# Expert weights stored by the host in the order in which each 2 MB transfer reads them

## The chip, the cores and the metric

The kernel runs on one core of one Trainium2 chip. Its engines are TensorE (PE: matmuls; PEld: the loads of its stationary operand), VectorE (DVE), ScalarE (ACT), GpSimd (POOL) and SyncE (SP). SP and POOL issue the transfers (DMAs), and 16 DMA engines carry them out. The metric is the time of one execution on the device in microseconds (us), the median over several runs; lower is better.

## The reference

Two transformer blocks run one after the other on 512 tokens of width 1024 in fp32. The first ends in a mixture of experts, which is where the change lies:

```
logits = xt @ w_router + b_router             # 512 tokens, 32 experts
top_v, top_e = lax.top_k(logits, 4); top_w = softmax(top_v)
# the 2048 (token, expert) rows are sorted by expert, padded per expert to blocks of 128
def expert_block(tok, e):
    xb = xt[tok]                              # 128 x 1024
    g = minimum(xb @ w_gate[e] + b_gate[e], 7)
    u = clip(xb @ w_up[e] + b_up[e], -7, 7)
    act = (u + 1) * (g * sigmoid(1.702 * g))
    return act @ w_down[e] + b_down[e]
y = zeros(512, 1024).at[row_tok].add(yb * row_w)
```

Each expert has three weights of 1024 x 1024 in fp32, 4 MB each. The second block has its own mixer and then a layer that fetches, for every token, 128 rows of 8 KB from a table of 16,384 by computed indices; it is the last stage of the kernel.

## The kernel before

The program is a row of stages. In `experts` (line 1018) a loop runs over the blocks of 128 routed rows; these inputs make 36. Each engine has a loop of its own, and they meet at semaphores.

For a block, PE computes gate and up in four units u of 8 matmuls (line 1121): u = 0 is gate, columns 0 to 511; u = 1 up, the same columns; u = 2 and 3 gate and up for columns 512 to 1023. The weights of a unit lie in `wgu[:, u]`, 128 partitions x 8 x 512 fp32, 2 MB in all, 16 KB per partition. After them come the transposes of the activation (line 1126), the transposes that turn the next block's rows `xg` (line 1107), and the down projection in two halves (line 1137) out of `wd[:, 0]` and `wd[:, 1]`, again 2 MB each. DVE and ACT do bias, clamp, sigmoid and products between.

There is one buffer for each of the six weight pieces. SP refills it as soon as PE has read it for this block (`s_mm[u]`), so a load has most of a block's time until its next use. A semaphore per buffer (`s_w[u]`) holds PE until it has landed. SP issues in this order: the four of `wgu` (line 1061), the two biases (lines 1064 and 1065, 512 KB each), the two of `wd` (line 1069), the down bias (line 1071). The host's arrays are as in the reference, so partition p of a gate or up piece is gathered from 8 rows of the weight (k x 128 + p), 2 KB of each; of a down piece from 4 rows, 4 KB of each.

POOL has a chain of small transfers for each block. It scatters the 128 finished rows of 4 KB (`e_yb`, line 1097) and waits until they have landed; then it loads the row table (line 1086) and the indices of the coming block (line 1089), waits for the indices, and gathers 128 rows of 4 KB into `e_xg` (line 1076). PE waits for that gather ahead of line 1107.

After the experts, the stage `combine` (line 1202) loads the scattered rows: `c_y` in four transfers of 2 MB, 16 KB in one piece per partition (line 1224).

Of the kernel before, what the change touches and what calls it, by code (L numbers as in the profile page):

```python
# [13 lines left out]
P = 128  # L14
T = 512
NT = T // P
D = 1024
KD = D // P
W = 512
# [14 lines left out]
NE, TOPK = 32, 4  # L34
# [983 lines left out]
def experts(nc, A, K, dram, ident, mod, x, ps, blocks):  # L1018

    with ExitStack() as ctx:  # L1020
        def sb(name, shape, dt=F32):
            return ctx.enter_context(nc.sbuf_tensor("e_" + name, shape, dt))

        def sem(name):
            return take(nc, "e_" + name)

        wgu = sb("wgu", [P, 4, KD, W])
        wd = sb("wd", [P, 2, KD // 2, D])
# [12 lines left out]
        s_w = [sem(f"w{u}") for u in range(6)]  # L1041
# [9 lines left out]
        with nc.Block() as block:  # L1051
            @block.sync
            def _(sp):
                nb = sp.value_load(blocks[0:1, NBLK:NBLK + 1], min_val=1, max_val=NBLK)
                with sp.Fori(0, NBLK) as i:
                    with sp.If(i < nb):
                        e = sp.value_load(blocks[0:1, bass.ds(i, 1)], min_val=0, max_val=NE - 1)
                        for u in range(4):
                            w = A["w_up" if u % 2 else "w_gate"][bass.ds(e, 1)]
                            sp.wait_ge(s_mm[u], i + 1)  # L1060
                            sp.dma_start(wgu[:, u], w.rearrange("e (k p) n -> p (e k) n", p=P)[:, :, (u // 2) * W:(u // 2 + 1) * W]
                                         ).then_inc(s_w[u], 16)
                        sp.wait_ge(s_act, i * 2 + 1)
                        sp.dma_start(bgu[:, 0, :], A["b_gate"][bass.ds(e, 1)].broadcast_to([P, D])).then_inc(s_bgu, 16)
                        sp.dma_start(bgu[:, 1, :], A["b_up"][bass.ds(e, 1)].broadcast_to([P, D])).then_inc(s_bgu, 16)
                        for u in range(2):
                            w = A["w_down"][bass.ds(e, 1)].rearrange("e (k p) n -> p (e k) n", p=P)
                            sp.wait_ge(s_mm[4 + u], i + 1)
                            sp.dma_start(wd[:, u], w[:, 4 * u:4 * u + 4, :]).then_inc(s_w[4 + u], 16)
                        sp.wait_ge(s_y, i + 1)  # L1070
                        sp.dma_start(bd[:, :], A["b_down"][bass.ds(e, 1)].broadcast_to([P, D])).then_inc(s_bd, 16)

# [1262 lines left out]
```

## Time and profile before

| | |
|---|---|
| median of 3 runs | 4891.05 us (4889.86 to 4891.41) |
| the profiled execution | 4888.82 us, span of its trace 4887.1 us |
| PE busy | 4101.2 us (84% of the span) |
| DVE / ACT / POOL busy | 1858.0 / 701.1 / 813.0 us |
| matmuls on the `wgu` weights | 2304, 997.3 us busy |
| matmuls on the `wd` weights | 1152, 512.4 us busy |
| transfers, whole kernel | 363,917 packets, 1245.03 MB, 255 GB/s |
| weight transfers of the expert stage | 72 gate + 72 up + 72 down, 2048 KB each |

Busy time is the time in which an engine had an instruction under way; what an engine waited for stands apart. A packet is one piece moved by one DMA engine. "DMA share" is the mean busy share of the 16 engines; it can come out slightly over 1 in a short stretch. "Landing" is the time from the issue of a transfer until all of it is there. [...]

### The profile page before, as it was taken

Reading aid. Unit: us, or ns where it says so; the run is one execution under the profiler, and the core shown is the slowest. Engines: PE = TensorE matmul, PEld = TensorE weight load, DVE = VectorE, ACT = ScalarE, POOL = GpSimd, SP = SyncE. Lnnn points to the kernel's source line nnn. Section 1 sums busy time; section 2 is a strip of 40 time slices with the busy share of each in tenths; the row PEclk is TensorE's granted clock in tenths of the full one; section 3 lists DMA queues with packets and bytes.
Section 4 is the critical chain, followed back from the end, with each engine's and each line's share of the span. In section 5 each row is a group of like instructions: output and inputs, shape, how many; then the busy total and the mean of one; then the engine's idle time right before and its main releaser. Section 6 shows DMA issues by size and latency. Waiting matters only on the chain. (4 is left out here: it accounts for less than half of the span.)

```text
span 4887.1 us, 33598 instructions
## 1 busy us (share of the span) xinstructions
PE 4101.2 (84%) x10884; PEld 2003.7 (41%) x10884; DVE 1858.0 (38%) x3983; ACT 701.1 (14%) x1559; POOL 813.0 (17%) x821
## 2 busy tenths in 40 slices
PE   7689999489999999999992984897967777777777
PEld 3235544244444444444441543674423333333332
DVE  1501222412222222222224025443066676676765
ACT  0001221011111111011110111111122222222221
POOL 0000000100000000000000003000044444444442
PEclk9799999699999999999996986557989899999998
DMA  9751122099999999999974100002089999999997
GB/s 327 201 102 68 55 71 95 18 385 351 351 342 350 344 343 350 348 345 343 351 280 168 52 5 0 0 1 103 18 348 421 421 421 421 421 419 419 403 420 310
DMA packets 363917, 1245.03 MB, mean 255 GB/s; under 512 B 24663, under 2 KB 26007, under 8 KB 297376
## 3 DMA queue, kind: packets, MB, share of 16 engines
q1 hardware_dynamic: 271552, 652.07, 37.0%
q0 software_dynamic: 92256, 591.59, 30.6%
q8 instruction: 57, 0.93, 0.1%
q14 instruction: 52, 0.43, 0.0%
HBM read 1212.48 MB, written 31.20 MB: 254 GB/s over the span
## 5 line engine op out<-in xcount | busy, mean ns | idle before, releaser
L2083 PE MATMUL ps<-q_uv,q_dg 128*128 128x512 f32 x2048 | 1002.7, 647 | 324.7 <-ACT q_dg L2109 324.7
L1121 PE MATMUL ps<-e_wgu,e_xT 128*128 128x512 f32 x2304 | 997.3, 593 | 1.2 <-ACT e_xT L1145 1.2
L2083 PEld LDWEIGHTS ps<-q_uv,q_dg 128*128 128x128 f32 x2048 | 412.6, 207 | 914.2 <-issue 914.2
L2194 DVE SCALAR_TENSOR_TENSOR mod<-q_uv,mix 128x1024 f32<-128x1024 f32 x512 | 627.3, 1225 | 394.4 <-DMA q_uv<-in_peer_uv,q_picks 393.8
L2067 POOL DMA_INDIRECT q_uv<-in_peer_uv,q_picks x512 | 590.1, 1153 | 867.5 <-PE ps L2083 669.4
L1121 PEld LDWEIGHTS ps<-e_wgu,e_xT 128*128 128x128 f32 x2304 | 438.6, 190 | 553.8 <-issue 553.8
L1137 PE MATMUL ps<-e_wd,e_aT 128*128 128x512 f32 x1152 | 512.4, 598 | 24.3 <-ACT e_aT L1157 24.3
L1137 PEld LDWEIGHTS ps<-e_wd,e_aT 128*128 128x128 f32 x1152 | 212.9, 190 | 275.4 <-issue 241.1
L498 PE MATMUL ps<-hT,ring 128*128 128x512 f32 x640 | 283.1, 600 | 15.7 <-ACT qkv L617 14.2
L1196 DVE TENSOR_TENSOR e_yb<-ps,e_bd 128x1024 f32<-128x1024 f32 x36 | 44.1, 1224 | 489.3 <-PE ps L1137 489.3
L1097 POOL DMA_INDIRECT scratch_y<-e_yb,e_row x36 | 35.6, 989 | 1042.1 <-DVE e_yb L1198 1011.1
L1185 DVE TENSOR_TENSOR e_ut<-ps,e_bgu 128x512 f32<-128x512 f32 x72 | 49.8, 691 | 404.8 <-PE ps L1121 404.8
L498 PEld LDWEIGHTS ps<-hT,ring 128*128 128x128 f32 x640 | 121.2, 192 | 162.4 <-issue 161.5
L1154 ACT ACTIVATE e_sg<-e_gt 128x512 f32<-128x512 f32 x72 | 45.3, 629 | 970.7 <-DVE e_gt L1183 970.7
L1182 DVE TENSOR_TENSOR e_gt<-ps,e_bgu 128x512 f32<-128x512 f32 x72 | 49.8, 691 | 346.4 <-PE ps L1121 286.4
L2109 ACT ACTIVATE q_dg<-ident,q_w 128x128 f32<-128x128 f32 x512 | 163.6, 390 | 60.1 <-DVE q_w L2208 59.8
L238 PE MATMUL ps<-mod_ring,cB 128*128 128x512 f32 x320 | 144.8, 613 | 25.6 <-DMA mod_ring<-in_w_ada 25.6
L2103 ACT ACTIVATE q_ap<-q_ap 128x4 f32<-128x4 f32 x128 | 26.3, 205 | 957.0 <-DVE mod L2194 957.0
L1344 PE MATMUL ps<-p_ring,p_hT 128*128 128x512 f32 (+1 forms) x352 | 132.1, 538 | 0.7 <-ACT p_hT L1361 0.7
L498 PE MATMUL ps<-ring,hT 128*128 128x512 f32 x256 | 113.6, 604 | 0.7 <-ACT hT L581 0.7
L1926 PE MATMUL ps<-r_mT,r_ring 128*128 128x512 f32 x256 | 112.4, 602 | 0.7 <-ACT r_mT L1943 0.7
L238 PEld LDWEIGHTS ps<-mod_ring,cB 128*128 128x128 f32 x320 | 63.3, 198 | 106.5 <-issue 106.3
(412 smaller groups left out, 3504.1 us busy)
## 6 DMA issues: line engine op xcount, KB each, us to landing
e_wgu<-in_w_gate SPq DMA_DIRECT2D x72, 2048.0 KB, 9.7
e_wgu<-in_w_up SPq DMA_DIRECT2D x72, 2048.0 KB, 9.1
e_wd<-in_w_down SPq DMA_DIRECT2D x72, 2048.0 KB, 9.5
ring<-in_w_in SPq DMA_DIRECT2D x15, 2048.0 KB, 8.1
mod_ring<-in_w_ada SPq DMA_DIRECT2D x12, 2048.0 KB, 9.9
mod_ring<-in_w_mod SPq DMA_DIRECT2D x12, 2048.0 KB, 7.9
e_bgu<-in_b_gate SPq DMA_DIRECT2D x36, 512.0 KB, 6.9
e_bgu<-in_b_up SPq DMA_DIRECT2D x36, 512.0 KB, 9.1
```

What stands on the lines that cost most here:

```text
L238: last = nc.tensor.matmul(ps[:, g % 4, :], cB[:, v, k, :], ring[:, n % NB, k, :], start=(k == 0), stop=(k == KD - 1))
L498: last = nc.tensor.matmul(ps[:, j, :], lhs, rhs, start=(k == 0), stop=(k == kt - 1))
L1121: last = nc.tensor.matmul(ps[:, u, :], xT[:, k, :], wgu[:, u, k, :], start=(k == 0), stop=(k == KD - 1))
L1137: last = nc.tensor.matmul(ps[:, 5 + c, :], aT[:, 4 * hf + k, :], wd[:, hf, k, c * W:(c + 1) * W], start=(hf == 0 and k == 0), stop=(hf == ...
L1182: link(dve.tensor_tensor(gt[:, hf], ps[:, 2 * hf, :], bgu[:, 0, cols], ALU.add))
L1185: link(dve.tensor_tensor(ut[:, hf], ps[:, 2 * hf + 1, :], bgu[:, 1, cols], ALU.add))
L1344: last = nc.tensor.matmul(ps[:, m % 8, 0:rhs.shape[1]], lhs, rhs, start=(k == 0), stop=(k == KD - 1))
L1926: last = nc.tensor.matmul(ps[:, m % 8, :], ring[:, n % NB, k, j * P:(j + 1) * P], mT[:, k, :], start=(k == 0), stop=(k == KD - 1))
L2067: pool.indirect_dma_start(out=uv[:, n % NR, :, :].rearrange("p a d -> p (a d)"), out_offset=None, in_=A["peer_uv"], in_offset=bass.Indirec ...
L2083: last = nc.tensor.matmul(acc(t)[:, c, :], dg[:, n % ND, :], uv[:, n % NR, 1, c * W:(c + 1) * W], start=first, stop=last_one)
L2109: act.activation(dg[:, n % ND, :], ident[:, :], ACT.Copy, scale=w[:, k % 2, j:j + 1]).then_inc(s_dg, 1)
L2194: dve.scalar_tensor_tensor(junk[:, n % 2, :], uv[:, n % NR, 0, :], 1.0, h3[:, k // PH, :], ALU.mult, ALU.mult, accum_out=ap[:, k % 2, j:j ...
```

## The change

The host stores the expert weights in the order in which the kernel's transfers want them. The gate and up weights become one array `w_in_exp` of [32 experts, 4 units, 128 partitions, 4096], the down weights `w_out_exp` of [32, 2 halves, 128, 4096]. Each of the six loads of a block then reads 16 KB in one piece for each partition. Sizes, buffers, semaphores, the order of issue and all arithmetic stay as they are.

```
-                            w = A["w_up" if u % 2 else "w_gate"][bass.ds(e, 1)]
+                            w = A["w_in_exp"][bass.ds(e, 1)].rearrange("e u p n -> p (e u) n")
                             sp.wait_ge(s_mm[u], i + 1)
-                            sp.dma_start(wgu[:, u], w.rearrange("e (k p) n -> p (e k) n", p=P)[:, :, (u // 2) * W:(u // 2 + 1) * W]
+                            sp.dma_start(wgu[:, u].rearrange("p k n -> p (k n)"), w[:, u, :]
                                          ).then_inc(s_w[u], 16)
...
-                            w = A["w_down"][bass.ds(e, 1)].rearrange("e (k p) n -> p (e k) n", p=P)
+                            w = A["w_out_exp"][bass.ds(e, 1)].rearrange("e u p n -> p (e u) n")
                             sp.wait_ge(s_mm[4 + u], i + 1)
-                            sp.dma_start(wd[:, u], w[:, 4 * u:4 * u + 4, :]).then_inc(s_w[4 + u], 16)
+                            sp.dma_start(wd[:, u].rearrange("p k n -> p (k n)"), w[:, u, :]).then_inc(s_w[4 + u], 16)
...
+    halves = [np.asarray(inputs.pop(n)).reshape(NE, KD, P, 2, W).transpose(0, 3, 2, 1, 4) for n in ("w_gate", "w_up")]
+    inputs["w_in_exp"] = np.stack(halves, 2).reshape(NE, 4, P, KD * W)
+    inputs["w_out_exp"] = np.asarray(inputs.pop("w_down")).reshape(NE, 2, 4, P, D).transpose(0, 1, 3, 2, 4).reshape(NE, 2, P, 4 * D)
```

The instructions of PE, DVE, ACT and POOL are the same, in the same order. On SP, in the loop over blocks of the expert stage, the loads of `wgu` read as follows (ISA is a register instruction or a wait; the last number of a DMA is its shape):

```order
 L1060 REGISTER_ALU
 L1061 ISA
-L1061 DMA e_wgu<-in_w_gate 128x8x512
-L1061 DMA e_wgu<-in_w_up 128x8x512
+L1061 DMA e_wgu<-in_w_in_exp 128x4096
 L1061 ISA
-L1061 DMA e_wgu<-in_w_gate 128x8x512
-L1061 DMA e_wgu<-in_w_up 128x8x512
+L1061 DMA e_wgu<-in_w_in_exp 128x4096
+L1061 ISA
+L1061 DMA e_wgu<-in_w_in_exp 128x4096
```

The loads stand where they stood; one more small instruction comes ahead of some of them, three in a block.

## Rows read from the trace of the kernel before

**Rows 1.** Busy time by stretch, 1030 to 2580 us (x: count)

```profile
core 0: us, PE busy (x) PEld busy (x) DVE busy (x) ACT busy (x) POOL busy (x), PEclk, DMA share, GB/s
1030.00:2580.00 1550.00, 1522.20 (x3938) 701.20 (x3936) 354.55 (x562) 168.12 (x246) 109.71 (x141) 1.00 0.94 341
```

**Rows 2.** Waits of PE, 1030 to 2580 us: us in total, times, longest

```profile
PE ps L1137 <- ACT e_aT L1157: 24.3, 36, 0.7
```

**Rows 3.** Timeline of PE, one block: start us, us, engine, line

```profile
1301.52 27.63 PE L1121 MATMUL ps<-e_wgu,e_xT 128*128 128x512 f32 x64
...
1345.48 27.63 PE L1121 MATMUL ps<-e_wgu,e_xT 128*128 128x512 f32 x64
...
1373.39 1.04 PE L1107 MATMUL ps<-ident,e_xg 128*128 128x128 f32 x8
```

**Rows 4.** Timeline of SP's issues in that block

```profile
1352.68 0.38 SPq L1061 DMA_DIRECT2D e_wgu<-in_w_gate  x1
1359.41 0.37 SPq L1061 DMA_DIRECT2D e_wgu<-in_w_up  x1
1366.41 0.37 SPq L1061 DMA_DIRECT2D e_wgu<-in_w_gate  x1
```

**Rows 5.** DMA issues of the page: count, KB each, median us to landing

```profile
e_wgu<-in_w_gate SPq DMA_DIRECT2D x72, 2048.0 KB, 9.7
e_wgu<-in_w_up SPq DMA_DIRECT2D x72, 2048.0 KB, 9.1
e_wd<-in_w_down SPq DMA_DIRECT2D x72, 2048.0 KB, 9.5
```

**Rows 6.** Timeline of POOL in that block (idle before, and what ended it)

```profile
1348.78 0.99 POOL L1097 DMA_INDIRECT scratch_y<-e_yb,e_row  x1 [28.58 <-DVE e_yb L1198]
...
1358.39 0.55 POOL L1089 DMA_DIRECT2D e_idx<-scratch_i_slots  x1 [0.17 <-issue]
1363.35 1.00 POOL L1076 DMA_INDIRECT e_xg<-scratch_h,e_idx  x1 [4.41 <-DMA e_idx<-scratch_i_slots]
```

**Rows 7.** The gathers of line 1076

```profile
DMA to landing us min/median/max: 4.3/5.8/7.5
```

**Rows 8.** DMA, 2590 to 2620 us: packets by size, queue, issues

```profile
DMA packets 865, 9.45 MB, mean 315 GB/s; under 512 B 96, under 2 KB 96, under 8 KB 352
...
q1 hardware_dynamic: 864, 9.44, 78.2%
...
c_y<-scratch_y SPq DMA_DIRECT2D x4, 2048.0 KB, 14.6
```

**Rows 9.** Busy time by stretch: experts, the load of y, broadcast loads

```profile
1356.00:1360.00 4.00, 4.00 (x10) 1.71 (x9) 0.58 (x1) 0.00 (x0) 1.14 (x2) 1.00 1.05 404
...
2602.00:2606.00 4.00, 0.00 (x0) 0.00 (x0) 3.89 (x4) 0.00 (x0) 0.00 (x0) 0.50 1.02 438
...
2648.00:2652.00 4.00, 0.00 (x0) 0.00 (x0) 0.00 (x0) 0.00 (x0) 0.00 (x0) 0.50 1.10 297
```

**Rows 10.** Timeline of PE, start of the expert stage

```profile
987.98 1.97 PE L1107 MATMUL ps<-ident,e_xg 128*128 128x128 f32 x8 [43.06 <-DMA e_xg<-scratch_h,e_idx]
```

**Rows 11.** Timeline of POOL, start of the expert stage

```profile
980.41 1.00 POOL L1076 DMA_INDIRECT e_xg<-scratch_h,e_idx  x1 [1.60 <-DMA e_idx<-scratch_i_slots]
```

**Rows 12.** DMA, 985 to 986 us: packets, MB, share, by queue

```profile
q0 software_dynamic: 63, 0.26, 65.8%
q1 hardware_dynamic: 68, 0.14, 36.4%
```

**Rows 13.** Busy time by stretch, PE's first matmuls of the stage

```profile
986.00:990.00 4.00, 1.97 (x8) 1.57 (x8) 0.00 (x0) 0.01 (x1) 0.55 (x1) 0.50 1.01 364
```

**Rows 14.** The index loads of line 1089

```profile
DMA to landing us min/median/max: 1.8/3.9/5.1
```

**Rows 15.** The scatters of line 1097

```profile
DMA to landing us min/median/max: 3.3/7.9/8.4
```

**Rows 16.** The weight loads into e_wgu

```profile
DMA to landing us min/median/max: 7.9/9.5/24.5
```

**Rows 17.** POOL's small loads of line 1313, beside 24 KB pieces

```profile
DMA to landing us min/median/max: 8.4/9.9/10.3
```

**Rows 18.** Busy time by stretch, the last stage

```profile
3700.00:4887.00 1187.00, 906.67 (x1858) 373.02 (x1856) 807.68 (x2038) 255.63 (x696) 523.94 (x453) 0.92 0.98 407
```

## The prediction

> **What bounds the kernel now.** I read the busy time by stretch first, because the change touches only the expert stage, 988 to 2577 us of a span of 4887.1. From 1030 to 2580 us PE is busy for 1522.20 of 1550 us at the full granted clock, while the 16 DMA engines are busy for 0.94 of the time at 341 GB/s [rows 1]. Two resources are thus nearly full, and the question is which one sets the pace. The list of waits answers it: in these 1550 us PE waited for one thing only, the copy of the transposed activations on ACT, 36 times and 24.3 us in all; no wait for a transfer stands in it [rows 2]. The timeline of PE agrees: block of 128 rows follows block at 1345.48 - 1301.52 = 43.96 us [rows 3]. PE bounds the stage and DMA is hidden.
>
> How deep it is hidden comes from two times. The first weight buffer is refilled at 1352.68 [rows 4], lands some 9.7 us later [rows 5] at 1362.4, and is read by the next block at 1345.48 + 43.96 = 1389.44: 27 us of cover. A faster weight transfer has nothing to give here, and one that took 27 us longer would cost nothing either.
>
> The cover of the small transfers is thin. POOL runs a chain of three per block, each waiting for the one before: it scatters the result of the last block, loads the next indices, and gathers the next 128 rows. They are issued at 1348.78, 1358.39 and 1363.35 [rows 6]. Gathers land after 5.8 us at the median [rows 7], so this one at 1369.15; PE turns those rows at 1373.39 [rows 3]. Slack: 4.2 us. This is the term that decides.
>
> **The change, part by part.** 216 transfers of 2 MB (72 + 72 + 72) are replaced by 216 of the same size, into the same buffers and behind the same waits. The gate and up transfers read 1024 pieces of 2 KB each, the down transfers 512 of 4 KB; all now read 128 of 16 KB. PE, DVE, ACT and POOL keep their instructions; SP gets three small register instructions more per block, which are hidden, since SP waits for PE between two issues some 7 us apart and spends 0.38 us on one [rows 4].
>
> *Rate of the weights.* The trace has a transfer of the new kind: after the experts, four transfers of 2 MB fetch y with 16 KB in one piece per partition. 864 packets moved 9.44 MB, 352 of them under 8 KB; the other 512 carry the 8.39 MB, so 16 KB each [rows 8]. They run at 438 GB/s at a busy share of 1.02 (429 per full share) against 404 at 1.05 (385) in the expert stage [rows 9]. A 2 MB transfer alone would go from 2.097 / 385 = 5.45 us to 4.9 us. Six per block save some 3.4 us of the DMA engines' 43.96, so their share falls from 0.94 to about 0.86. On the path this is worth 0, by the cover above.
>
> *The first block.* Here a DMA is waited for. PE starts at 987.98 after 43.06 us of idle that the gather ended; the gather was issued at 980.41 [rows 10, 11], amid the first weight loads, and took 7.5 us against 4.3 for the quickest [rows 7]. How two queues share is seen from 985 to 986 us: 63 packets of the gather's queue (4 KB each) and 68 of the weights' (2 KB each) [rows 12], one for one. Each of 16 engines has 8 gather packets. Beside a 2 KB packet (2 KB x 16 / 385 GB/s = 0.085 us) one costs 0.17 + 0.085, 2.0 us for eight. Beside a 16 KB packet (4.9 us / 8 = 0.61) one costs 0.17 + 0.61, 6.2 us for eight: +4.2. Lower bound: the gather slips in unhindered, -3.2 (7.5 to 4.3). Upper bound: it also waits for one whole transfer of 4.9 us, +9. I take +4, since one-for-one is what the row shows for this very transfer. Everything behind shifts with it, once. The weights that PE needs then are queued earlier and land faster; they are not late. PE's clock stands at 0.50 of full speed, the lower of its two levels, when it starts [rows 13]; its recovery moves with it and costs the same.
>
> *The 35 later gathers.* Their chain is exposed to the same sharing. Today index load, gather and scatter take 3.9, 5.8 and 7.9 us at the median against 1.8, 4.3 and 3.3 at the least [rows 7, 14, 15], so 8.2 us of the chain is already contention. With 16 KB packets each 4 KB row that meets a weight packet loses 0.61 - 0.085 = 0.53 us more; eight rows 4.2. But the weights now leave gaps. The quickest weight load lands 7.9 us after its issue [rows 16], 5.45 of that data, so some 2.5 us lie around the data. By that the load issued at 1359.41 lands near 1359.41 + 2.5 + 4.9 = 1366.8, and the next, issued at 1366.41, moves its first packets a us or two after that. The gather, issued by 1364.35 and ready about a us later (the quickest index load, 1.8 us, bounds that), needs 8 x 0.17 = 1.4 us once the weights pause: it lands near 1368 to 1369, as today. The scatter meets the tail of a weight load and the 512 KB bias load in 4 KB pieces, which the change leaves as it is. I take 0 for all 35. Bounds: no gain is possible (slack only grows); at worst scatter and gather are both interleaved in full (4.2 each) and the index load loses two packets (1.2), 9.6 against a slack of 4.2, so PE waits 5.4 us, 35 times: +189.
>
> The row for how queues share is again the 63 packets against 68 [rows 12]: at 2 and 4 KB the engines turn after every packet. [...]
>
> *Sum.* Profiled run 4888.82 (span 4887.1 and 1.7 outside it); + 4 + 0 = 4892.8. The median of the runs is 4891.05, 2.2 above the profiled one. Forecast 4891 + 4 = 4895 us.
>
> **Rivals.**
> 1. *The chain of small transfers becomes the bound* (slower). Place: PE's turn of the gathered rows in each block. It decides once the chain is more than 4.2 us longer. With half of the 4 KB rows interleaved (4 x 0.53 = 2.1 for scatter and for gather) and 1.2 on the index load, 5.4, PE waits 1.2 us in each of 35 blocks: +42, with the first block 4937. For it: beside transfers of 24 KB pieces, POOL's small loads landed after 8.4 to 10.3 us [rows 17], against 1.8 for the quickest index load. Against it: the gaps between weight loads, and that those 24 KB pieces came 3 MB at once. Chance 0.14.
> 2. *Small transfers queue behind whole weight loads* (slower). Each of the three then waits 4.9 us: 14.7, less the 8.2 that is contention already, is +6.5, PE waits 6.5 - 4.2 = 2.3 us x 35 = 81, with the first block 4976. For it speaks rows 17, against it the alternation in rows 12. Chance 0.06. [...]
> 3. *Large pieces run slower* (slower). The slowest saturated stretch of large pieces moved 297 GB/s at 1.10 [rows 9], a broadcast of one region. A block moves 341 x 43.96 = 15.0 MB; at 297 that takes 50.5 us, +6.5 a block, 234 in all: 5125. The 438 GB/s of rows 9 speak against it. Chance 0.02.
> 4. *Something outside the stage moves, or the first gather gains* (either side). The expert-row fetch of the last 1187 us is bound by DMA at 407 GB/s [rows 18], and its table may lie elsewhere in memory once the host's arrays differ; 1% of it is 12 us, 4879 or 4903. Nothing in the profile says that it would. Chance 0.08, 0.05 of it faster.
> 5. *Nothing at all*: the first gather is not delayed. 4888 to 4892, inside the forecast's own range.
>
> **How the numbers follow.** The forecast with rival 5 holds 0.70; its own range is 4888 (first gather -3) to 4900 (+9). A change below 0.2%, 10 us, can't be told from none here. Same: 0.70, and 0.03 from rivals 1 and 4 where they stay small: 0.73. Faster: 0.05, from rival 4. Slower: 0.22. The range leaves out about 0.05 below and reaches up into rival 1, to its first price: 4886 to 4937.
>
> **What would show it.** In the expert stage 128 packets of 16 KB per weight load, the weights' median landing under 9 us, DMA share near 0.86, block after block at 43.96 us and no wait of PE for a transfer after the first block. The wait before 987.98 should grow to about 47 us and the first gather's landing to 11 or 12. The median landing of the later gathers should stay within 2 us of 5.8. I am wrong if PE waits for e_xg in later blocks, if the period is above 44, or if the last stage's time differs by more than some us.

## The result: slower by 0.25 to 0.46%, inside the range, above the point

| | median us (lowest to highest) | beside it, kernel before | ratio, 95% interval |
|---|---|---|---|
| changed kernel | 4913.70 (4900.71 to 4926.90, 7 runs) | 4891.41 (7 runs) | 1.0046 (1.003 to 1.0063) |
| the same kernel, measured again | 4906.50 (4901.10 to 4924.01, 10 runs) | 4893.76 (20 runs) | 1.0025 (1.0016 to 1.0034) |

The forecast was 4895 in a range of 4886 to 4937, "same" at 0.73 and "slower" at 0.22. It came out slower: by 22 us in the first comparison and by 13 in the second, where +4 had been forecast. The runs of the changed kernel also spread over 26 us and, measured again, over 23 (nine of those ten lie within 7.4); those of the kernel before spread over 6 and 9. What the change costs differs from run to run.

The profiled execution has a span of 4907.4 us against 4887.1, so 20.3 more. First the busy time of the expert stage and the saturated start of it (PEclk is PE's granted clock as a share of full speed; the traces of this case record only 0.50 and 1.00, and a row gives the mean):

```profile
core 0: us, PE busy (x) PEld busy (x) DVE busy (x) ACT busy (x) POOL busy (x), PEclk, DMA share, GB/s
1030.00:2580.00 1550.00, 1519.32 (x3919) 701.07 (x3918) 352.64 (x560) 167.53 (x245) 109.71 (x140) 1.00 0.91 341
998.00:1006.00 8.00, 6.76 (x13) 3.06 (x12) 0.00 (x0) 2.36 (x3) 1.02 (x2) 0.59 1.01 428
```

Against [rows 1] the DMA share fell from 0.94 to 0.91 at the same 341 GB/s; where the DMA engines are full they now move 428 GB/s at 1.01, against 404 at 1.05 [rows 9]. The weights did get somewhat faster. The issues of the page say the same, against [rows 5]:

```profile
e_wgu<-in_w_in_exp SPq DMA_DIRECT2D x144, 2048.0 KB, 9.3
e_wd<-in_w_out_exp SPq DMA_DIRECT2D x72, 2048.0 KB, 8.9
```

Now what PE waits for. The waits of PE from 940 to 2620 us (us in total, times, longest):

```profile
PE ps L1107 <- DMA e_xg<-scratch_h,e_idx: 54.2, 4, 47.1
PE ps L1137 <- ACT e_aT L1157: 24.3, 36, 0.7
```

The gather was waited for once before, now four times. The timeline of PE gives the four places; the last two rows show how the work behind one late gather runs:

```profile
996.78 1.97 PE L1107 MATMUL ps<-ident,e_xg 128*128 128x128 f32 x8 [47.13 <-DMA e_xg<-scratch_h,e_idx]
...
1426.74 1.09 PE L1107 MATMUL ps<-ident,e_xg 128*128 128x128 f32 x8 [0.67 <-DMA e_xg<-scratch_h,e_idx]
...
1650.80 1.97 PE L1107 MATMUL ps<-ident,e_xg 128*128 128x128 f32 x8 [4.11 <-DMA e_xg<-scratch_h,e_idx]
...
2095.65 1.09 PE L1107 MATMUL ps<-ident,e_xg 128*128 128x128 f32 x8 [2.28 <-DMA e_xg<-scratch_h,e_idx]
2096.58 8.73 PE L1137 MATMUL ps<-e_wd,e_aT 128*128 128x512 f32 x16
```

The first wait grew from 43.06 [rows 10] to 47.13 us. The three later ones are 7.06 us, but they cost more: the block after the wait of 4.11 begins 51.04 us after the one before it, 7.08 over the usual 43.96; the others lost 4.13 and 0.82. Together 12.0; the first block of the stage took 0.2 less, which leaves 11.8. Of the 5.0 us that the three blocks lost beyond their waits, 4.8 lie in the two in which the granted clock fell (the means of its rows are 0.50 and 0.68 in one, 0.61 in the other); the third, at 1.00 behind its wait, lost 0.15. The rows around the wait of 4.11 us:

```profile
1640.00:1650.00 10.00, 6.69 (x19) 2.98 (x17) 3.47 (x7) 1.22 (x2) 0.27 (x1) 0.99 0.91 334
1650.00:1654.00 4.00, 3.20 (x10) 2.44 (x11) 0.00 (x0) 1.07 (x2) 0.00 (x0) 0.50 0.97 391
1654.00:1658.00 4.00, 4.00 (x8) 1.60 (x7) 0.00 (x0) 0.00 (x0) 0.00 (x0) 0.68 0.59 230
```

PE's granted clock was 0.99 on average up to 1650 us, most of the wait included, 0.50 (the lower level) right after it, and 0.68 on average in the next 4 us. After 2.28 us of idle the same happened in part: the clock was 0.61 on average from 2096 to 2100 us and 0.96 in the next 4, and the 16 matmuls behind the wait took 8.73 us, against 7.10 in a block without a wait.

So the 20.3 us of this execution are: 4.1 for the first gather, 11.8 for the late gathers with their clock, 4.7 that had been lost before the stage began (PE's last matmuls ahead of the stage ended at 943.03 + 1.89 before, 947.76 + 1.90 now), and -0.3 behind the stage. The 4.7 fall ahead of everything that the change touches, and a kernel whose median equals that of before shows such a difference too: in small_pieces, below, these matmuls began at 949.64, 6.6 us later than before.

### The profile page after: what moved, and what is told of

It reads as the page before. It is cut to its first block and busy times, and to the rows that moved or that the text cites. A ratio compares the mean times of both kernels' runs of the same rounds, so it can differ in the third digit from the quotient of the medians.

```text
span 4907.4 us, 33706 instructions
## 1 busy us (share of the span) xinstructions
PE 4118.1 (84%) x10884; PEld 2015.9 (41%) x10884; DVE 1859.3 (38%) x3983; ACT 700.9 (14%) x1559; POOL 813.2 (17%) x821
```

## Why a late gather is late: one packet for one

POOL's timeline of the block that lost most, from the scatter on:

```profile
1621.92 0.99 POOL L1097 DMA_INDIRECT scratch_y<-e_yb,e_row  x1 [27.76 <-DVE e_yb L1198]
1631.61 0.59 POOL L1086 DMA_DIRECT2D e_row<-scratch_i_slots  x1 [8.70 <-issue]
1632.36 0.55 POOL L1089 DMA_DIRECT2D e_idx<-scratch_i_slots  x1 [0.17 <-issue]
1639.26 1.01 POOL L1076 DMA_INDIRECT e_xg<-scratch_h,e_idx  x1 [6.34 <-DMA e_idx<-scratch_i_slots]
```

Scatter to gather took 17.34 us here, 14.57 in [rows 6]: the scatter landed some 0.8 us later and the index load 1.9. SP's timeline has the third weight load of this block at 1639.55, 0.3 us behind the gather. In [rows 4, 6] the gather is 3 us ahead of it. Here the two met.

Of the three late gathers, this one and the one of the 2.28 us wait were issued within 0.8 us of the third weight load. The third, of the 0.67 us wait, was not: it was issued 2.3 us ahead of the load, as several were that landed after 5.2 to 6.6 us; it took 10.1. Its rows came in two parts. DMA of the changed kernel, 1418 to 1421 us and 1421 to 1426:

```profile
q0 software_dynamic: 134, 0.49, 44.4%
```

```profile
q1 hardware_dynamic: 102, 1.65, 93.8%
q0 software_dynamic: 9, 0.03, 2.3%
```

All but 0.03 MB of the gather, that is 8 rows of 4 KB, went in the first 3 us; those 8 took 5 us more, beside weights. So being issued late is one way to be late, and a few rows that fall behind the weights are another.

What a meeting costs is seen cleanest in the first gather, which always meets one. DMA of the changed kernel, 989 to 995 us:

```profile
DMA packets 262, 2.52 MB, mean 420 GB/s; under 512 B 16, under 2 KB 16, under 8 KB 139
...
q1 hardware_dynamic: 139, 2.02, 80.7%
q0 software_dynamic: 123, 0.50, 20.5%
```

Without the 16 tiny packets, 123 weight packets of 16 KB (2.02 MB) and 123 gather packets of 4 KB (0.50 MB) ran in these 6 us. [Rows 12] had 68 against 63 in 1 us. Equal sums alone would also come out if each of the 16 engines moved 8 rows of the gather and then 8 packets of a weight load. The stretch from 991 to 995 us alone speaks against that:

```profile
DMA packets 167, 1.68 MB, mean 419 GB/s; under 512 B 4, under 2 KB 4, under 8 KB 85
...
q1 hardware_dynamic: 86, 1.34, 81.7%
q0 software_dynamic: 81, 0.33, 20.2%
```

That is 82 weight packets (without the 4 tiny ones) against 81, and in the four single microseconds 22 to 21, 20 to 17, 19 to 24 and 21 to 19 (weights first). The two queues go packet for packet as before, and a packet of the weights is now eight times the size, 16 KB against 2. That each engine turns after every packet, as the prediction has it, is read from such counts; the trace does not say which engine moved a packet. The landings, against [rows 7, 14, 15, 16], of the gathers, the index loads, the scatters and the weights into `e_wgu`:

```profile
DMA to landing us min/median/max: 4.4/6.4/11.5
DMA to landing us min/median/max: 1.9/4.5/6.0
DMA to landing us min/median/max: 3.3/7.8/8.7
DMA to landing us min/median/max: 7.7/9.3/22.7
```

The medians moved by 0.6 us at most; the longest gather grew from 7.5 to 11.5 us.

Theory A: a small transfer that meets weight packets is delayed by the size of one packet, eight times per engine for the gather's 128 rows. Rivals: the place of the weights in memory (B), any 16 KB load delays the chain (C), the cost lies outside the gathers (D), the waits are rare accidents that have nothing to do with meeting a load (E), only the largest packets hurt (F), or any merging hurts alike (G).

## Experiments

Stage time below is from the first PE row on `e_xg` (line 1107) to the last group on `e_wd` in the profile; that of before is 2569.39 - 987.98 = 1581.41 us, of the changed kernel 2589.98 - 996.78 = 1593.20.

| kernel | median us | kernel before beside it | ratio, 95% interval | first wait | later waits of PE for a gather | stage |
|---|---|---|---|---|---|---|
| small_pieces | 4894.02 | 4893.82 | 1.0004 (0.9995 to 1.0012) | 43.4 | 0 | 1581.09 |
| down_only | 4893.26 | 4893.82 | 1.0001 (0.9992 to 1.001) | 43.0 | 3, 2.8 us | 1584.88 |
| gate_up_only | 4905.19 | 4893.82 | 1.0024 (1.0015 to 1.0032) | 48.0 | 3, 7.4 us | 1593.14 |
| pieces_8k | 4897.06 | 4893.76 | 1.0011 (1.0001 to 1.002) | 45.0 | 3, 5.1 us | 1590.98 |
| changed_again | 4906.50 | 4893.76 | 1.0025 (1.0016 to 1.0034) | 47.0 | 5, 16.3 us | 1606.85 |
| gather_early | 4897.60 | 4893.82 | 1.0009 (1.0 to 1.0018) | 46.8 | 0 | 1581.23 |
| early_and_held | 4893.72 | 4894.18 | 0.9996 (0.9987 to 1.0005) | 43.0 | 0 | 1581.28 |
| before_gather_early | 4895.41 | 4894.18 | 1.0003 (0.9994 to 1.0012) | 43.2 | 0 | 1581.27 |
| changed_gather_late | 5051.40 | 4894.18 | 1.0314 (1.0299 to 1.033) | 47.0 | 35, 112.6 us | 1736.70 |
| before_gather_late | 4957.92 | 4894.18 | 1.0124 (1.0108 to 1.0139) | 43.2 | 35, 54.6 us | 1642.96 |

The waits and the stage are those of one profiled execution of each kernel, the medians those of 4 to 12 runs.

**small_pieces: the new arrays, the old size of packet.**

```
-    sp.dma_start(wgu[:, u].rearrange("p k n -> p (k n)"), w[:, u, :]
+    sp.dma_start(wgu[:, u], w[:, u, :].rearrange("p (k n) -> p k n", k=KD)[:, :, 0:W]
```

(the same for `wd` with k=4, and the host pads each piece by 64 numbers)

> The host arrays of the changed kernel, but each piece of 2 KB (4 KB of the down weights) is followed by 256 bytes that no transfer reads, so that the loads again move pieces of 2 and 4 KB out of nearly contiguous memory. Theory A (the size of one packet is what delays the small transfers): 4888 to 4896 us as before, first gather landing in 7 to 8 us, no later wait of PE for a gather. Theory B (the place of the weights in memory, or the new arrays): the time of the changed kernel, 4901 to 4927 us, with waits in some blocks.

Time, first wait and stage are those of before. The memory layout costs nothing that can be told; B falls. (The weights lie nearly in one piece here, but for the gaps of 256 bytes.)

**down_only and gate_up_only: one half of the change each** (the lines of `wgu`, or those of `wd`, as before).

> Only the down weights are read in 16 KB pieces, gate and up in pieces of 2 KB. Theory A (the gathers collide with the third gate/up load, the first gather with the first loads): 4888 to 4897 us, no wait of PE for a gather after the first block, first gather as before at 7.5 us. Theory C (any 16 KB load delays the chain, the scatter beside the second down load too): scatter landing well over 8.4 us at the most and waits in some blocks, 4900 us or more.

> Only gate and up weights are read in 16 KB pieces, the down weights in pieces of 4 KB. Theory A: as the changed kernel, 4901 to 4927 us; first gather landing in 11 to 12 us, PE waits for a gather in one to five of the later blocks. Theory C: clearly less than the changed kernel loses, near 4898 us.

The down weights alone cost nothing in the median, whose interval reaches to 0.1% or 5 us. But three short waits appeared (2.8 us, and 3.5 us more stage), and a scatter took up to 10.8 us against 8.4 [rows 15]: what C named does happen, on a small scale, and A was too absolute. The gate and up weights alone show the long first wait and the lost stage time of the changed kernel; C is not needed for the bulk. One of the three waits there, of 2.01 us, followed a scatter that took 11.3 us, while its gather landed after 5.6. So a late scatter alone can make PE wait.

**pieces_8k: half the packet.**

```
+    sp.dma_start(wgu[:, u].rearrange("p (h k) n -> p h (k n)", h=2), w[:, u, :].rearrange("p (h n) -> p h n", h=2)[:, :, 0:2048]
```

(the same for `wd`, and the host pads each 8 KB by 64 numbers)

> The changed kernel's arrays with 256 bytes after each 8 KB, so that each weight load moves two pieces of 8 KB per partition. Theory A by the size of the packet: beside packets of 0.31 us the first gather takes 8 x (0.17 + 0.31) = 3.8 us instead of 2.0 (2 KB) and 6.2 (16 KB), so it lands in 9.2 to 9.5 us, 1.8 later than before, and fewer later gathers are late: 4894 to 4902 us. Rival F (only the largest packets hurt, by a step): as before, 7.5 to 7.9 us and 4894 us. Rival G (any merging hurts alike): 11.3 us and over 4903 us.

From the gather's issue to PE's start: 987.98 - 980.41 = 7.57 us with 2 KB, 989.46 - 979.97 = 9.49 with 8 KB, 996.78 - 985.36 = 11.42 with 16 KB. The expected steps were +1.8 and +4.2, the measured ones are +1.9 and +3.9. The cost of the first gather goes with the size of the packet; F and G fall. The median lies in the expected range, barely above no change. The later gathers do not follow the size: three were waited for, as many as in the profile of the changed kernel, though fewer were expected, and the landings of all gathers are slower at the median than with 16 KB (8.3 against 6.4 us):

```profile
DMA to landing us min/median/max: 4.8/8.3/9.9
```

Why is open.

**changed_again.**

> The changed kernel itself once more, on another chip perhaps and beside more runs of the kernel before. Theory A: again slower by 0.25 to 0.5%, runs spread over 15 us or more since the number of blocks that miss the gap differs from run to run: 4903 to 4920 us. If it were 4895 or less, the first comparison would have been an accident.

Slower again. Its profile (span 4922.3) is of the slowest of the ten runs, with five late gathers instead of three; all five were issued within 0.6 us of the third weight load. Of the 14.9 us between the two profiles 13.7 lie in the stage (1606.85 against 1593.20). So the number of late gathers makes a spread of this size; the other runs have no profile that could show it.

**gather_early: more slack for the gather.** POOL issues index load and gather for the block after next as soon as PE has turned the rows before, and the scatter after them (the table of slots is one block longer):

```
 with pool.Fori(0, NBLK) as i:
     with pool.If(i < nb):
+        with pool.If(i < nb - 1):
+            pool.wait_ge(s_xg, i * 16 + 32)
+            ...  # load idx of block i + 2, wait for it
+            pool.wait_ge(s_xt, i * 2 + 4)
+            gather()
         ...      # scatter of block i, wait for it, then load the row table of block i + 1
```

> The changed kernel, with GpSimd's chain turned round: the index load and the gather for the block after next are issued as soon as PE has turned the rows before them, ahead of the scatter. The gather then has over 30 us of slack instead of 4.2. Theory A: all waits after the first block are gone; what stays is the first gather (+4 us) and its clock: 4892 to 4899 us, range between runs as small as before (6 us). Theory D (the slower runs come from outside the expert stage): no change from the changed kernel, runs still spread over 20 us.

All later waits are gone and the stage is back at 1581.23 us; 4897.6 in a range of 12 us, where the runs of the kernel before beside it spread over 13. The long first wait stays. So the loss inside the stage was that of PE's waits for gathers; D falls. The gathers themselves are not quick here: they land after 8.8 us at the median and 11.3 at most, which now has slack.

**early_and_held: and the first gather freed.** In addition SP holds the second weight load, and with it those behind it, until the first gather has landed:

```
 sp.wait_ge(s_mm[u], i + 1)
+if u == 1:
+    sp.wait_ge(s_xg, 16)
```

> The changed kernel with GpSimd's chain turned round (gather ahead of scatter) and, besides, SyncE holding the second and all later weight loads until the first gather has landed. Theory A: the first gather then meets one weight load instead of four and lands in at most 8 us instead of 11.3 to 11.6; PE waits some 43 us before its first rows instead of 47; no later wait for a gather. 4888 to 4895 us, as the kernel before, within noise. Theory D (something else than the gathers costs the rest): 4897 us, as without the hold.

The first wait is back at 43.0 us and the time at that of before. With 16 KB pieces and both exposures closed the kernel is neither faster nor slower than before, to within some 6 us by the interval: the faster weights are worth nothing that can be told.

**before_gather_early: the control.**

> The kernel before with only GpSimd's chain turned round. Theory A: no gather is waited for there, so nothing is to be had, 4890 to 4897 us, same. If the turned chain had a gain or a cost of its own, it would show here.

No effect, as expected: the turned chain has no gain or cost of its own that can be told.

**changed_gather_late and before_gather_late: issue every gather with the load.** POOL waits until PE has read the third buffer, and issues the gather with its refill:

```
 pool.wait_ge(s_xt, i * 2 + 2)
+pool.wait_ge(s_mm[2], i + 2)
```

> The changed kernel; each gather is held until PE has read the third gate/up buffer, so that it is issued together with the refill of that buffer and always meets it. Theory A (packets of both queues alternate one for one, 8 rows of a gather against 8 packets of 16 KB): gather lands about 4 us later than in the same edit of the kernel before, PE waits 3 to 5 us in each of 35 blocks and its clock falls each time, some 6 to 8 us a block: 5100 to 5180 us. Rival E (the waits of the changed kernel are rare accidents that have nothing to do with meeting a weight load): same time as the same edit of the kernel before.

> The kernel before with the same hold of the gather. Theory A: beside 2 KB packets the gather loses under 1 us, landing in 6 to 8 us after issue against a slack of some 7: PE waits 0 to 1 us a block, 4891 to 4930 us. Rival E: same as the changed kernel with this edit.

Both expectations were missed. The kernel before was to end at 4930 at most and took 4958: with 2 KB packets every block waited, 1.56 us on average (54.6 / 35), and the kernel lost 64 us. The changed kernel was to take 5100 or more and took 5051: 157 us lost, 93 more than with 2 KB. 58 of the 93 are longer waits (112.6 - 54.6); the other 35 show as busy time of PE, 1567.5 us for 3952 matmuls from 1030 to 2730 us at a granted clock of 0.97 on average, against 1532.6 us for 3954 from 1030 to 2640 us at 1.00 in the kernel before with the same hold.

The waits are not all alike: 21 of the 35 are 1.7 to 2.1 us, seven are 3.4 to 4.6 and seven 6.1 to 6.9. Waits of PE in the changed kernel, in the kernel before, and the gathers' landings in the changed one and in the one before:

```profile
PE ps L1108 <- DMA e_xg<-scratch_h,e_idx: 159.6, 36, 47.0
```

```profile
PE ps L1108 <- DMA e_xg<-scratch_h,e_idx: 97.8, 36, 43.2
```

```profile
DMA to landing us min/median/max: 4.2/8.4/13.3
DMA to landing us min/median/max: 4.5/8.0/8.7
```

So theory A's price, some 4 us more for each of the 35, was not paid: the median gather took 0.4 us longer than beside 2 KB packets, and the longest 4.6 longer. What the large packets made here is a tail, 13.3 us against 8.7.

One of the long waits, 6.81 us, ended at 1324.21. From 1315 to 1319 us 0.50 MB of its gather moved, 120 of the 128 rows, beside 78 packets on the weights' queue. The last 8 rows took from 1319 to 1324 us, beside 130. The middle of that, 1320 to 1323 us, has 79 packets on the weights' queue and 4 on the gather's:

```profile
q1 hardware_dynamic: 79, 1.28, 99.7%
q0 software_dynamic: 4, 0.02, 1.3%
```

So packet for packet, as counted in the first gather, does not hold for these last rows. Again 8 rows came last, as in the gather that took 10.1 us. Why they did is not shown: the trace does not say which engine moved a packet.

Rival E (accidents that have nothing to do with meeting a load) falls: with the same hold the two kernels differ by 93 us. Why the gather gets through quickly in 21 blocks and falls behind in 14 stays open.

## Why the prediction was right where it was, and wrong where not

- **PE bounds the stage, the weights are hidden:** right. PE's waits show none for weights before or after; the blocks without a late gather still follow at 43.96 us, and early_and_held shows no value of the faster loads.
- **Rate of the weights:** the rate was nearly right (428 GB/s at a share of 1.01, so 424 per full share, 429 forecast). The share was mis-sized (0.91, forecast 0.86), and so was the landing of the gate and up weights (9.3 us, forecast under 9; the down weights 8.9). The sum took 385 GB/s for all six loads; with the down weights alone in large pieces the share is 0.93, so little was to be saved there. Nothing hangs on it.
- **First gather, +4:** right: 4.07 in the profile, and +1.9 of 1.8 for half the packet. The term was one for one, 0.53 us for each of 8 rows, and the packet counts (123 against 123) bear out the one for one. The 8 rows are 128 over 16 engines; the trace does not show how they were shared out.
- **The 35 later gathers, 0:** this step failed. It placed the gather by median times into a pause of the weights, some 3 us ahead of the next load, and took the median for all blocks. The median held (6.4 us, within the 2 us of 5.8 that were allowed); the tail decides. Three and five of 35 gathers were waited for in the two profiles, for 7.1 and 16.3 us, where 0 had been put. Seven of these eight were issued within 0.8 us of the third load, 16.9 to 18.2 us behind their scatter, against 14.57 in [rows 6]; the eighth was held up by its last 8 rows. Why scatter and index load are late in just these blocks is open. The prediction named the place in rival 1, but let that rival hold in every block, at 1.2 us each. What happens is rare and dear: up to 4.2 us of wait, and 3 more behind the wait of 4.11, at a granted clock of 0.50 and then 0.68. The clock was no term of the forecast for a wait inside the stage.
- **Rival 2 (behind whole weight loads)** did not happen: 82 packets against 81 from 991 to 995 us and the steps of +1.9 and +3.9 contradict it for the first gather.
- **Rivals 3 and 4** did not happen: 16 KB pieces are not slow, and the 20.3 us split up without the last stage (-0.3 behind the expert stage).
- **The chances:** "same" was held too high, since a change below 10 us was forecast from a sum in which the term of the 35 gathers can't be negative. That the time lies inside the range is owed to the room that the range left for rival 1 and not to the sum.

## What to carry to other kernels

The weight loads were hidden here, and larger pieces gained nothing (early_and_held: 4893.72 us against 4894.18); the first gather, moved packet for packet with them, took 3.9 us longer from its issue to PE's start. So beside a hidden transfer look for the small transfers whose landing is waited for, and take their slack not at the median but in the worst block (the gathers here took 6.4 us at the median, and 11.5 in the block that lost most). Eight rows times the estimated duration of one weight packet priced the first gather well (+4.2 for a measured +3.9); it did not price the later ones: issued with the load, the median gather lost 0.4 us against the same hold with small packets, and the slowest 4.6, more than that price. If large pieces are wanted, first give the small chain slack (here: gather ahead of scatter, 4897.6 us instead of 4906.5), and keep the first, unhidden transfer clear of bulk loads (4893.7 us).

## What was not expected of the hardware

- After a wait of 4.11 us in a stretch in which PE was otherwise busy, its granted clock was 0.50 instead of 0.99, and the block lost 7.08 us in all; with a wait of 2.28 us it lost 4.13, with one of 0.67 us 0.82.
- Packets of 16 KB on one queue and 4 KB on another went 123 to 123 in 6 us, whatever their bytes: the queue of small packets got 0.50 of 2.52 MB.
- A gather of 128 rows can be all but done and still land late: 8 of its rows took 5 us behind the rest, beside 16 KB packets.
